# Two merges of expert results rebuilt: order of the first by tile, last one scaled at eviction and summed on TensorE

## The reference, cut to what matters

```python
h = modulate(x, shift_f, scale_f)          # rows that go to the experts
y = hier_moe(h, ...)                       # two experts per token, weighted
x = layer_norm(ALPHA * x + g_f * y, ln2_g, ln2_b)     # ALPHA = (2 * DEPTH) ** 0.25
# next layer begins:
h = modulate(x, shift_a, scale_a)          # a second layer norm on the new x
u = h @ w_in + b_in                        # the value columns "nv" come first
```

## Time and profile before

| | |
|---|---|
| three runs | 2724.19, 2727.01 and 2728.3 us; median 2727.01 |
| the profiled execution | 2721.01 us, its span 2719.2 us |
| TensorE busy | 2481.5 us, 91% of the span |
| VectorE, ScalarE, GpSimd busy | 927.6, 626.8, 346.5 us |
| granted TensorE clock, mean | 0.966 of full speed |
| DMA | 604.39 MB, mean 222 GB/s |
| chain that ended last | PE 68%, DMA 13%, DVE 10%, ACT 3% |

### The profile page before, as it was taken

The page is one execution under the profiler, slowest core; times in us unless marked ns, Lnnn a source line. Parts: engine busy times, 40 slices in busy tenths (PEclk is TensorE's granted clock), DMA queues, the critical chain, the costliest instruction groups (busy, mean ns, idle before and its releaser), DMA issues.

```text
span 2719.2 us, 32992 instructions
## 1 busy us (share of the span) xinstructions
PE 2481.5 (91%) x12757; PEld 1531.8 (56%) x12757; DVE 927.6 (34%) x1764; ACT 626.8 (23%) x1174; POOL 346.5 (13%) x409
## 2 busy tenths in 40 slices
PE   5999999999999889989986999999999899989984
PEld 3768656788885533434332768567887433434331
DVE  3335466622224820001005534556332820001003
ACT  2331345622220111101102421446331011101100
POOL 1241000001111220100002520000011220100101
PEclk7999999999999999999998999999999989999997
DMA  9571001322217599999996560004333799999994
GB/s 285 191 260 47 7 1 13 77 64 68 59 55 209 230 390 421 421 421 417 421 421 238 196 212 22 7 1 87 98 99 123 295 384 420 420 420 402 420 419 153
DMA packets 238331, 604.39 MB, mean 222 GB/s; under 512 B 67328, under 2 KB 143504, under 8 KB 188640
## 3 DMA queue, kind: packets, MB, share of 16 engines
q1 hardware_dynamic: 210786, 528.65, 51.7%
q0 software_dynamic: 24512, 63.13, 6.6%
q10 hardware_dynamic: 2880, 10.49, 1.0%
HBM read 585.70 MB, written 38.16 MB: 229 GB/s over the span
## 4 chain that ended last, share of the span: by engine, by line
PE 68%; DMA 13%; DVE 10%; ACT 3%; SPq 3%; issue 2%; POOL 0%; DVEq 0%; ACTq 0%; POOLq 0%
PE slot L1130 21%; PE abank L708 18%; PE vbank L708 11%; DMA arena<-in_w_up_e 6%; PE slot L1028 3%; DMA arena<-in_w_down_e 3%; PE vbank L904 2%; SPq L2684 2%; DMA arena<-in_w_in 1%; DVE nmx L1545 1%; DVE stat L1265 1%; PE vbank L700 1%; PE abank L791 1%; PE vbank L851 1%; PE slot L931 1%
## 5 line engine op out<-in xcount | busy, mean ns | idle before, releaser
L1130 PE MATMUL slot<-arena 128*64 128x512 f32 (+2 forms) x3264 | 827.4, 619 | 81.9 <-DMA arena<-in_w_up_e 58.5
L1130 PEld LDWEIGHTS slot<-arena 128*64 128x64 f32 (+2 forms) x3264 | 297.7, 147 | 557.8 <-issue 549.7
L708 PE MATMUL abank<-round,round 128*128 128x512 f32 (+1 forms) x1792 | 492.0, 355 | 5.8 <-DVE round L1362 2.4
L708 PEld LDWEIGHTS abank<-round,round 128*128 128x128 f32 x1792 | 318.3, 189 | 70.0 <-issue 14.3
L1896 DVE TENSOR_TENSOR arena<-slot,arena 128x512 f32<-128x512 f32 x76 | 52.6, 692 | 797.6 <-ACT arena L2217 503.1
L708 PE MATMUL abank<-hT_low,round 128*128 128x512 f32 (+1 forms) x896 | 317.9, 355 | 0.0
L708 PE MATMUL vbank<-round,round 128*128 128x512 f32 (+2 forms) x1312 | 307.1, 360 | 3.2 <-issue 2.0
L708 PEld LDWEIGHTS vbank<-round,round 128*128 128x128 f32 x1312 | 227.0, 189 | 38.4 <-issue 4.5
L708 PEld LDWEIGHTS abank<-hT_low,round 128*128 128x128 f32 x896 | 168.9, 188 | 23.8 <-issue 0.5
L1637 DVE TENSOR_TENSOR arena<-vbank,arena 128x512 f32<-128x512 f32 x72 | 43.4, 603 | 304.5 <-PE vbank L708 304.2
L1028 PE MATMUL slot<-arena 128*128 128x512 f32 x320 | 138.4, 593 | 3.4 <-POOL arena L2380 3.4
(11 more groups left out here) (299 smaller groups left out, 2703.6 us busy)
## 6 DMA issues: line engine op xcount, KB each, us to landing
arena<-in_w_gate_e SPq DMA_DIRECT2D x128, 1024.0 KB, 27.0
arena<-in_w_up_e SPq DMA_DIRECT2D x128, 1024.0 KB, 27.0
arena<-in_w_down_e SPq DMA_DIRECT2D x128, 1024.0 KB, 28.0
arena<-in_w_ada POOLq DMA_DIRECT2D x80, 512.0 KB, 4.9
arena<-in_w_in SPq DMA_DIRECT2D x48, 512.0 KB, 4.2
arena<-in_w_in SPq DMA_DIRECT2D x8, 2048.0 KB, 14.7
h_rows<-arena ACTq DMA_DIRECT2D x20, 512.0 KB, 8.0
arena<-y_rows SPq DMA_DIRECT2D x20, 512.0 KB, 8.0
```

The costliest lines, as they stand in the source:

```text
L708: last = pe.matmul(to, x, y, start=(k == 0 and q == 0), stop=(k == len(terms) - 1 and q == 2))
L1130: last = pe.matmul(to[at, cols], x[:, at], w[:, at_w, :], start=first, stop=final)
```

## The change

- **Value weights.** The chunk is loaded before the extra blocks, once the last weights in its place are used, and no longer between the loads of y. The extra blocks' buffers move to make room (`wg`, `wu`, `wd`). VectorE runs `value_lower` before the merge. The bias row `bnv` is loaded after the first four tiles of y.
- **First merge.** `merge_first` and `merge_last` become four steps (`merge_gain`, `merge_sum`, `merge_centre`, `merge_scale`), tile by tile. `nv_taken(t - 2)` stands where `nv_taken(t - 3)` stood, and VectorE does `tile_lower` for the last two tiles. GpSimd's order changes likewise; for tile 1 its `tile_lower(0)` stands between the two norms.
- **Clock products.** Ahead of the mixes TensorE issues `keep_clock` with 10 products in layer 0 and 5 in layer 1, after `share_ready`.
- **Last layer.** The gain row (`gf_row`, loaded with the rows of the router) is multiplied in when a block's down product is evicted, which VectorE now does in layer 1 in ScalarE's place, the last block and the extra ones too. TensorE adds ALPHA x by a product with `alpha_eye` (`scaled_rows`) into banks of each tile's own (`sums`), and the two rows onto it (`mix_on_rows`). VectorE takes the moments from PSUM and centres from there (`last_moments`, `last_centre`). The two gain rows are no longer loaded at the end of layer 1.

The diff, without the two places where only the awaited count of a row semaphore changes (`rows8_by`), and with most unchanged lines left out:

```diff
@@ -372,11 +372,13 @@
-        wg, wu, wd = [[ar3(kb + 48 * n, *shape) for n in range(2)] for kb, shape in
-                      ((0, (KD, FE)), (16, (KD, FE)), (32, (4, D)))]
+        wg, wu, wd = [[ar3(kb, *shape) for kb in two] for two, shape in
+                      (((0, 64), (KD, FE)), ((32, 80), (KD, FE)), ((48, 96), (4, D)))]
         t12 = [ar(104, D), ar(108, D)]
+        alpha_eye = ar(165, P)
+        gf_row = x_sb[:, 0, :]
@@ -508,6 +510,15 @@
+        def rows8_by(L):
+            return 16 * (NROWS8 * (L + 1) + (L + 1 == DEPTH))
+        def sums(n):
+            return ((slot[0][:, 0:512], slot[0][:, 512:1024]), (vbank[0][:, :], vbank[1][:, :]),
+                    (abank[0][:, :], abank[1][:, :]), (slot[1][:, 0:512], slot[1][:, 512:1024]))[n]
@@ -515,10 +526,10 @@
         def first_norm(n):
-            return 2 * n if n else 1
+            return 2 * n + 1
         def second_norm(L, n):
-            return min(2 * n + 3, 2 * len(qtiles(L)))
+            return 2 * n + 2
@@ -642,6 +653,20 @@
                                          yg[n % 4][k][:, half * 512:(half + 1) * 512], start=(k == 0), stop=(k == 1))
+                last.then_inc(mixed, 1)
+            def scaled_rows(L, n):
+                for half, to in enumerate(sums(n)):
+                    pe.matmul(to, alpha_eye, x_sb[:, qtiles(L)[n], half * 512:(half + 1) * 512], start=True, stop=False)
+            def mix_on_rows(L, n):
+                pe.wait_ge(g_in[n], 32 * (1 + sum(n < len(qtiles(k)) for k in range(L))))
+                for half, to in enumerate(sums(n)):
+                    for k in range(2):
+                        last = pe.matmul(to, share[n][k], yg[n][k][:, half * 512:(half + 1) * 512],
+                                         start=False, stop=(k == 1))
@@ -1233,9 +1258,19 @@
                 pe.wait_ge(share_ready, L + 1)
-                for n in range(4):
-                    mix(L, n)
-                if L + 1 == DEPTH:
+                pe.wait_ge(act_taken, len(agroups))
+                if L + 1 < DEPTH:
+                    keep_clock(slot[0], 10)
+                    for n in range(4):
+                        mix(L, n)
+                else:
+                    keep_clock(slot[0], 5)
+                    for n in range(3):
+                        scaled_rows(L, n)
+                    mix_on_rows(L, 0)
+                    scaled_rows(L, 3)
+                    for n in range(1, 4):
+                        mix_on_rows(L, n)
@@ -1266,30 +1301,56 @@
-            def merge_first(L, n):
+            def merge_gain(L, n):
+                c = 0 if qtiles(L)[n] >= CTX_TILES else 1
+                if n == 0:
+                    dve.wait_ge(rows12_in, 80)
+                dve.wait_ge(mixed, before(L) + n + 1)
+                dve.tensor_tensor(t12[n % 2], slot[n % 2][:, :], rows2[f"gf{c}"], ALU.mult).then_inc(t_ready, 1)
+            def merge_sum(L, n):
                 t = qtiles(L)[n]
-                c = 0 if t >= CTX_TILES else 1
                 T = t12[n % 2]
-                if n == 0:
-                    dve.wait_ge(rows12_in, 96 + 64 * L)
-                if n >= 2:
-                    dve.wait_ge(x_ready, before(L) + n - 1)
-                dve.wait_ge(mixed, before(L) + n + 1)
-                dve.tensor_tensor(T, slot[n % 2][:, :], rows2[f"gf{c}"], ALU.mult).then_inc(t_ready, 1)
-            def merge_last(L, n):
+            def merge_centre(L, n):
+            def merge_scale(L, n):
+                t = qtiles(L)[n]
                 dve.wait_ge(rstd_ready, merge_norm(L, n))
-                dve.scalar_tensor_tensor(x_sb[:, t, :], T, rstd[:, t:t + 1], rows2["ln_b"], ALU.mult, ALU.add
+                dve.scalar_tensor_tensor(x_sb[:, t, :], t12[n % 2], rstd[:, t:t + 1], rows2["ln_b"], ALU.mult, ALU.add
+            def last_moments(L, n):
+                t = qtiles(L)[n]
+                if n == 0:
+                    dve.wait_ge(rows12_in, 128)
+                dve.wait_ge(mixed, before(L) + n + 1)
+                for k, bank in enumerate(sums(n)):
+                    last = dve.bn_stats(stat[:, t, k, :], bank)
+                link(last)
+                dve.bn_aggr(mv[:, t, :], stat[:, t, :, :]).then_inc(stats_ready, 1)
+            def last_centre(L, n):
+                t = qtiles(L)[n]
+                dve.wait_ge(stats_ready, merge_norm(L, n))
+                for k, bank in enumerate(sums(n)):
+                    cols = slice(512 * k, 512 * k + 512)
+                    put = dve.scalar_tensor_tensor(t12[n % 2][:, cols], bank, mv[:, t, 0:1], rows2["ln_g"][:, cols],
+                                                   ALU.subtract, ALU.mult)
+                link(put)
@@ -1368,14 +1429,16 @@
+                    if L and t >= CTX_TILES:
+                        dve.wait_ge(x_in[t - 1], 80)
                     ps = take()
-                    if t == 0 and L == 0:
-                        dve.wait_ge(rows12_in, 16)
+                    if t == 0:
+                        dve.wait_ge(rows12_in, 96 if L else 16)
@@ -1410,19 +1473,20 @@
                 else:
-                    merge_first(L - 1, 0)
-                    merge_first(L - 1, 1)
+                    value_lower()
+                    merge_gain(L - 1, 0)
                     for t in range(NTILES):
-                        merge_last(L - 1, t)
+                        merge_sum(L - 1, t)
+                        merge_centre(L - 1, t)
+                        if t + 1 < NTILES:
+                            merge_gain(L - 1, t + 1)
+                        merge_scale(L - 1, t)
                         moments(x_sb[:, t, :], t, mv).then_inc(stats_ready, 1)
-                        if t == 0:
-                            value_lower()
-                        if t + 2 < NTILES:
-                            merge_first(L - 1, t + 2)
-                        if t >= 3:
-                            nv_taken(t - 3)
-                    nv_taken(NTILES - 3)
+                        if t >= 2:
+                            nv_taken(t - 2)
+                    tile_lower(NTILES - 2)
+                    tile_lower(NTILES - 1)
@@ -1895,6 +1959,11 @@
                                           ).then_inc(half_taken, 1)
+                    if part == "down" and half == 1 and L + 1 == DEPTH:
+                        dve.wait_ge(unit_used, mark["part_done", L, i, "down"])
+                        if blocks_to(L, i) > 1:
+                            dve.wait_ge(y_stored[i % 2], 16 * (blocks_to(L, i) - 1))
+                        dve.tensor_tensor(yb[i % 2], slot[1][:, :], gf_row, ALU.mult).then_inc(y_ready, 1)
@@ -1915,7 +1984,11 @@
                         dve.wait_ge(X["y_out"], j * 1 + 1)
-                        dve.tensor_copy(yb[0], slot[1][:, :]).then_inc(X["dve"], 1)
+                        if L + 1 == DEPTH:
+                            put = dve.tensor_tensor(yb[0], slot[1][:, :], gf_row, ALU.mult)
+                        else:
+                            put = dve.tensor_copy(yb[0], slot[1][:, :])
+                        put.then_inc(X["dve"], 1)
@@ -1925,14 +1998,16 @@
                         last = dve.tensor_scalar(share[n][k], ident, wtok[:, n, k:k + 1], None, ALU.mult)
+                if L + 1 == DEPTH:
+                    last = dve.tensor_scalar(alpha_eye, ident, ALPHA, None, ALU.mult)
                 if L + 1 == DEPTH:
-                    merge_first(L, 0)
-                    merge_first(L, 1)
+                    last_moments(L, 0)
                     for n in range(nq):
-                        merge_last(L, n)
-                        if n + 2 < nq:
-                            merge_first(L, n + 2)
+                        last_centre(L, n)
+                        if n + 1 < nq:
+                            last_moments(L, n + 1)
+                        merge_scale(L, n)
@@ -2215,7 +2290,7 @@
                         act.activation(am[i % 3], slot[0][:, n % 2 * FE:n % 2 * FE + FE], ACT.Sigmoid).then_inc(sgm_ready, 1)
-                    elif part == "down" and half == 1:
+                    elif part == "down" and half == 1 and L + 1 < DEPTH:
@@ -2310,9 +2385,10 @@
                 else:
-                    deviation(mv[:, 0, 1:2], rstd[:, 0:1])
-                    deviation(mv[:, 1, 1:2], rstd[:, 1:2])
                     for t in range(NTILES):
+                        deviation(mv[:, t, 1:2], rstd[:, t:t + 1])
+                        if t == 1:
+                            tile_lower(0)
@@ -2320,11 +2396,8 @@
                         st["r"] += 1
-                        if t:
+                        if 2 <= t < NTILES - 1:
                             tile_lower(t - 1)
-                        if t + 2 < NTILES:
-                            deviation(mv[:, t + 2, 1:2], rstd[:, t + 2:t + 3])
-                    tile_lower(NTILES - 1)
@@ -2653,6 +2726,8 @@
                     mod_row(rows[f"sh{v_}"], v_, 3).then_inc(rows8_in, 16)
+                if L + 1 == DEPTH:
```

(18 more changed lines are left out.)

## The result

| | before | after |
|---|---|---|
| runs, median | 2722.78 us (6 runs, 2719.47 to 2728.3) | 2735.11 us (6 runs, 2732.99 to 2738.73) |
| ratio, 95% | | 1.004 [1.003, 1.005] |
| profiled execution, its span | 2721.01, 2719.2 us | 2737.11, 2735.3 us |
| TensorE busy, VectorE busy | 2481.5, 927.6 us | 2506.1, 942.0 us |
| granted clock, mean | 0.966 | 0.966 |

The change costs 12.3 us by the medians. In a later set of runs it was 15.0 us: 2740.23 against 2725.28, 1.0062 [1.0043, 1.0081]. The forecast was +11.3.

What follows compares the result with a forecast made beforehand. With experts at the DMA limit (about 420 GB/s) and the rest at TensorE, it read the chain between them; 8.2 - 0.5 + 3.6 = +11.3 us on 2727.0 gives 2738.3 us, range 2728 to 2746 for 8 in 10.

Steps and rivals of the forecast that it cites:

- The walks: Engines walk 21 skipped extra blocks after the last planned block: 9.0 us on VectorE, 12 to 14 on TensorE.
- the first rival: Both layers: walks are short and clock products hide, so faster; -9.3 in all, 2717.7 us; chance 0.07 for over 0.2%.
- the published figure: Walk past skipped blocks: the skill's 108 ns per compare-and-branch would give 3.4 us, total about -4; the trace disagrees.
- Three to four times: Skipped blocks: whole walks in the trace were said to take this multiple of the skill's 3.4 us.
- Layer 0's start: Before layer 0's first merge: ten clock products stand ahead of mix after TensorE's walk, hiding nothing; +8.2 us.
- the low clock: TensorE's start from idle before the mixes: costs 1.7 us extra; in layer 0 clock products pay it instead of mix.
- y would be later: Layer 0: y may land later behind the value chunk, which costs nothing up to 1465.4.
- Layer 1's start: Before layer 1's merge: VectorE's walk delays the shares to 2680.0, then 30 TensorE instructions; VectorE starts at 2694.7, +10.7 us.
- The last merge: Layer 1: VectorE's four tiles take 19.0 us against 26.05, -7.1 us (-8 to -6); the store's 9.1 us stays.
- The first merge: Layer 0, first mix to "f" columns: value_lower's 4.4 us saved, mostly lost to the new order; -0.5 us, bounds -4.4 and +2.5.
- Hidden parts: Layer 1's VectorE evictions, the gf_row load and fewer broadcasts: each costs 0, at most 1.3 us.
- The sum: Whole kernel: 8.2 - 0.5 + 3.6 = +11.3 us, giving 2738.3 us.

Runs made afterwards that it cites:

- after_again: The changed kernel as it is, timed once more beside other kernels on one chip: 2740.23 against 2725.28 us, 1.0062.
- last_merge_only: The kernel before with the last layer's part of the change alone, no clock products, layer 0 as before: 2720.84 us, 0.9991.
- before_no_walk: The kernel before without the code of the skipped extra blocks on all engines: 2722.03 us, 0.9991.
- no_products: The changed kernel without the clock products ahead of the mixes in both layers: 2727.81 against 2724.78 us, 1.0013.
- shares_first: The changed kernel with VectorE building layer 1's shares before its walk: 2741.8 against 2724.78 us, 1.0059; again beside the changed kernel, 2740.14 against 2725.28.
- weights_early_only: The kernel before with the value weights' early load and early value_lower alone, old tile order, no clock products: 2720.34 us, 0.9991.

## Why the prediction was right, point by point

**The walks.** Right, and the step on which everything rested. In the changed kernel TensorE's ends at 1460.1 in layer 0, VectorE's runs 2683.1 to 2691.75 in layer 1. Taken out, the same change is 8 us faster than before, which is the first rival's kernel; it forecast -9.3.

The reading of the published figure was only half right. The Trainium skill, "Advanced Engine Details and Errata", Control Flow Timing, has about 108 ns for a compare-and-branch. TensorE's take 208 to 221 ns in the median, with single ones of 2 to 3 us, but VectorE's take 56 ns (21 of them) and 66 ns (10), less than the page has. VectorE's walk is long for another reason: its 65 recorded instructions sum to 3.8 of 9.0 us in layer 1 of the kernel before, and the rest lies between them. So counting branches can't price a walk. "Three to four times" 3.4 us holds for TensorE; VectorE's 9.0 us is 2.6 times it.

**Layer 0's start, +8.2.** Measured +10.0 (27.2 us) in the first profile of the changed kernel (after), +8.2 (25.4 us) in the second (after_again). TensorE begins as late after the last down product as before (11.87 against 12.02 us). The term that was too small in the first is the low clock. I had let the products pay only what mix had paid, 1.7 us. The stretches of after (us, then busy PE, PEld, DVE, ACT, POOL, PEclk, DMA share, GB/s), against the earlier trace rows:

```profile
1460.24:1467.10 6.86, 6.86 (x9) 2.87 (x10) 2.20 (x1) 0.00 (x0) 0.00 (x0) 0.57 1.00 389
1467.10:1472.02 4.92, 4.92 (x13) 2.26 (x12) 0.00 (x0) 0.00 (x0) 0.00 (x0) 1.00 0.40 160
```

The granted clock is 0.57, near the 1.2 GHz level, for 6.86 us, where it was for 2.99: nine instructions at about 0.76 us, so 3.0 us extra. In the second profile the 20 products took 10.32 us and not 11.78. The 1.7 us came from the one trace of the kernel before, the lowest of all: the first mixes of last_merge_only and before_no_walk pay about 3. Against their 18.7 and 19.0 us the two profiles give +6.4 to +8.5. That y would be later was right in its direction (+1.0 us, no_products) and in its price: nothing while the products stand there.

**Layer 1's start, +10.7.** Measured +11.9. `share_ready` comes 10.8 us after the last down product (11.0 forecast). Two terms were missing or small. TensorE's own walk, which I took to end well ahead because it did at 2676.3 in the kernel before, ends last, and TensorE starts 0.95 us after the shares; and the 30 instructions take 15.15 us, not 14.6. So the engine that holds this start in the changed kernel is not the one forecast. VectorE's walk ends less than 1 us earlier, which is why the number is near all the same. In last_merge_only, without the long branch, the forecast path is the true one. The missed walk decided one experiment (shares_first).

**The last merge, -7.1.** Measured -7.5: 18.57 us against 26.05, with 1.41 us for the two subtractions out of PSUM (1.4 forecast) and 1.29 for two bn_stats. The tail after it (store and end) was to stay at 9.1 and became 7.1. It is 6.8 to 7.8 in every kernel with the new merge, 9.0 to 9.2 in three with the old one but 7.3 in the fourth (before_no_walk). What takes it is open.

**The first merge, -0.5, bound +2.5.** Measured +3.5, and +5.0 in the second profile: beyond the bound, the worst step. The place and the kind were right: an idle stretch ahead of the first `nv` eviction, 5.78 us (4.6 forecast), the product ending 32.4 us after the first mix (30.6), the last moments at 61.7 (58). No single term is far out. The product took its 6.8 us (5.6 and 1.2 for the clock), but tile 1 was turned at 25.7 and not 23.7: `tile_lower(0)` took 2.96 us for 2.35 (+0.6), tile 1's norm 2.1 for 1.65 (+0.5), centring and transposes 2.8 for 2.3 (+0.5), and the first step began 0.3 later. The error in kind was the bound: I had priced the slow forms once, at the end, where each lies on the chain that VectorE then waits for, tile after tile (13.4 us in four waits; weights_early_only has 9.2 in two, with no tile's step behind them).

**Hidden parts, 0.** No eviction, row or broadcast shows in the expert stage: 479.0 us against 481.8, and 478.7 in weights_early_only, which has the old evictions.

**The sum.** +11.3 forecast, +12.3 and +15.0 measured. By the traces the terms were +10.0, +3.5, +11.9 and -9.5, so three costs were low by 1.2 to 4.0 us, the gain was low by 2.4, and unchanged stretches swing as much. The sign and the main mechanism (the walks) are shown; the closeness of the size is partly luck.

## What to carry to other kernels

Before filling a wait of one engine with cheap work, look at what its sequencer does there: a wait for data and a walk past skipped blocks look the same in the busy rows, and work put behind the walk hides nothing. Work that needs no result of a conditional block belongs ahead of it, on every engine of the chain at once: moved on VectorE alone it won nothing, since TensorE's walk ended as late. (No run moves it on both; taking both walks out won the 20 us.) And an early load pays only with the order that goes with it: the value weights loaded ahead shortened the first merge by 3.7 us, the tile by tile order built on them lengthened it by 8. And one trace's value for a start from idle is not its price: the same first mix took 5.1 to 6.7 us.

## What the runs showed of the hardware

A compare-and-branch takes 208 to 221 ns in the median on TensorE's weight sequencer and 56 or 66 ns on VectorE's. Walking past 21 skipped blocks took 9 to 12 us on VectorE and 11.7 to 15 us on TensorE, where the longest branch took 0.3 to 3.4 us; its length in layer 1 went with code elsewhere in the program. The scatter of the last 128 rows of y took 2.66 us in the three traces without the early value chunk and 5.9 to 6.1 us in the eleven where that load of 2 MB ran beside it. Two bn_stats of 512 columns took 1.29 us out of PSUM as out of SBUF; two subtractions of 512 columns out of PSUM took 1.41 us, where one of 1024 columns out of SBUF took 1.23 to 1.30 us. After some 12 us of idle time the first mix of layer 0 took 5.1 to 6.7 us, at a mean granted clock of 0.72 to 0.55.
